# Projecting 32 sample tokens through four column groups of TensorE, beside the first prompt tile

## What is computed

```python
D_MODEL, SEQ, DEC_BATCH, DEC_SEQ = 1024, 1024, 8, 4
u = rmsnorm(h, attn_pre_g)
qa, kva, qi, ki, wi, qb, kb, vb, g_a, g_b = jnp.split(u @ w_in, cuts, axis=-1)
qa = rope(qa.reshape(B, T, H_A, DH_A), pos)          # rope: [x1*cos - x2*sin, x1*sin + x2*cos]
kv_a = jnp.stack([rope(kva[:, :, 0], pos), kva[:, :, 1]], axis=2)
qi = rope(qi.reshape(B, T, N_IDX, D_IDX), pos)
ki = rope(ki.reshape(B, T, 1, D_IDX), pos)[:, :, 0]
qb, kb = rope(qb, pos), rope(kb, pos)                # as heads of 64 columns
# samples: indexer scores over 8192 cached keys + 4 new ones, top 256 of them
score = einsum('bqh,bqhs->bqs', wi * N_IDX**-0.5, relu(einsum('bqhd,bsd->bqhs', qi, kidx) * D_IDX**-0.5))
_, sel = lax.top_k(score, 256)
```

## Time and profile before

| | |
|---|---|
| median of three runs | 3236.38 us |
| the profiled execution | 3238.8 us, its span 3237.3 us |
| PE busy | 2876.3 us (89% of the span) |
| VectorE busy | 1461.4 us (45%) |
| ScalarE busy | 588.2 us (18%) |
| GpSimd busy | 678.3 us (21%) |
| moved by DMA | 708.73 MB, mean 219 GB/s |

### The profile page before, as it was taken

One profiled execution on the slowest core, in us unless ns is written; L12 is line 12 of the kernel. 1 busy time (PEld: TensorE's weight loads), 2 busy tenths in 40 slices (PEclk: granted clock), 3 DMA queues, 4 the chain that ended last, 5 costly groups with the idle time before them and its releaser, 6 DMA issues. The chain is left out here.

```text
span 3237.3 us, 69341 instructions
## 1 busy us (share of the span) xinstructions
PE 2876.3 (89%) x26593; PEld 2020.4 (62%) x26593; DVE 1461.4 (45%) x3004; ACT 588.2 (18%) x1308; POOL 678.3 (21%) x1192
## 2 busy tenths in 40 slices
PE   8998979998789669999978889999798799998698
PEld 4764534665466446666755567766566576675698
DVE  2337858996788354333343443323433632002211
ACT  2431112001566110101011110010100201001101
POOL 0131003001100001133332433333333333430000
PEclk9999989999899889999998999999899899999799
DMA  7575239422500757789888988888888896662586
GB/s 226 148 226 181 79 117 305 128 79 87 164 8 18 223 182 245 241 299 315 297 303 271 310 297 276 308 305 302 300 282 276 268 300 235 223 204 91 174 266 197
DMA packets 419892, 708.73 MB, mean 219 GB/s; under 512 B 67985, under 2 KB 230193, under 8 KB 419442
## 3 DMA queue, kind: packets, MB, share of 16 engines
q1 hardware_dynamic: 330674, 470.65, 44.5%
q0 software_dynamic: 75456, 232.86, 21.7%
q10 hardware_dynamic: 13440, 0.85, 0.3%
HBM read 660.01 MB, written 92.13 MB: 232 GB/s over the span
## 5 line engine op out<-in xcount | busy, mean ns | idle before, releaser
L1458 PE MATMUL sa_t<-tw_z,tw_w 128*128 128x304 f32 x2496 | 679.8, 428 | 14.8 <-DVE tw_z L1535 10.7
L1458 PEld LDWEIGHTS sa_t<-tw_z,tw_w 128*128 128x128 f32 x2496 | 470.5, 192 | 195.3 <-issue 44.4
L1736 POOL DMA_DIRECT2D sa_ring_v<-cache_b_kv x512 | 275.2, 537 | 1211.5 <-PE sa_o L1865 850.4
L1458 PE MATMUL sa_t<-tw_x,tw_w 128*128 128x304 f32 x1440 | 406.0, 438 | 43.4 <-DMA tw_w<-packed 37.8
L1976 DVE STREAM_TRANSPOSE sa_key_b<-sa_ring_k 128x2048 f32<-128x2048 f32 x128 | 294.9, 2307 | 263.9 <-PE sa_s L1798 194.1
L1458 PEld LDWEIGHTS sa_t<-tw_x,tw_w 128*128 128x128 f32 x1440 | 277.5, 197 | 151.5 <-issue 64.6
L414 PE MATMUL pr_acc<-pr_w,pr_u_t 128*128 128x512 f32 (+1 forms) x720 | 288.1, 548 | 3.8 <-DVE pr_row L574 3.7
L1737 POOL DMA_DIRECT2D sa_ring_va<-cache_a_kv x512 | 274.2, 536 | 54.1 <-issue 27.0
L874 PE MATMUL sel_g<-sel_u,sel_gw 128*128 128x352 f32 x768 | 227.5, 459 | 0.0
L1798 PE MATMUL sa_s<-sa_key_b,sa_q_pad 32*32 32x256 f32 x8192 | 191.9, 416 | 26.1 <-DVE sa_key_b L1976 19.3
L874 PEld LDWEIGHTS sel_g<-sel_u,sel_gw 128*128 128x128 f32 x768 | 145.8, 190 | 81.9 <-issue 0.8
(11 more groups left out here) (336 smaller groups left out, 3499.7 us busy)
## 6 DMA issues: line engine op xcount, KB each, us to landing
sa_ring_k<-cache_b_kv SPq DMA_DIRECT2D x512, 256.0 KB, 4.0
sa_ring_v<-cache_b_kv POOLq DMA_DIRECT2D x512, 256.0 KB, 6.3
tw_w<-packed SPq DMA_DIRECT2D x228, 512.0 KB, 6.5
tp_w<-packed SPq DMA_DIRECT2D x76, 512.0 KB, 4.3
sa_ring_ka<-cache_a_kv SPq DMA_DIRECT2D x512, 64.0 KB
sa_ring_va<-cache_a_kv POOLq DMA_DIRECT2D x512, 64.0 KB, 6.2
packed<-w_gate_up POOLq DMA_DIRECT2D x44, 512.0 KB, 13.7
tw_w<-packed SPq DMA_DIRECT2D x48, 256.0 KB, 7.5
```

Source lines behind the costliest of these rows:

```text
L1458: ins = pe.matmul(bank[:, 0:self.width], self.w[:, at % self.SLOTS, k - lo, :], moving[:, k, :], start=(k == 0), stop=(k == depth - 1))
L1736: pool.dma_start(ring_v[:, n % RING, :], rows_of(cache_b, page, 1)).then_inc(v_in[n // 4 % 2], 16)
```

## The change

Tile 0 is no longer padded to 128 rows in the projection.

- **Four column groups.** Each chunk of 512 columns is cut into four of 128. For each of the eight slices of the contraction, four matmuls with a stationary operand of 128 x 32 (the 32 tokens) go to the array's column groups at 0, 32, 64 and 96, and stream 128 columns each. The result of one chunk is a block of 128 partitions (group, token) x 128 columns; the four large chunks fill one bank of 512 columns, borrowed from the selection's `dots[0]`. The chunk of 68 columns is written to a corner of the bank `once`.
- **One tile to rotate and turn.** VectorE rotates all four chunks at once with a cos/sin table repeated over the four groups (`trig_new`, four more small loads), and copies the unrotated values back over one block. PE turns four blocks and one of 64 columns instead of 16; ScalarE copies them out in five copies. The rows and heads of the 32 tokens leave in eight and four stores instead of four and one.
- **Tile 1 gets its own input buffer.** Its `x` and `ple` are loaded into the `rank` buffer (free until the ranking) right behind tile 0's, ahead of the weights. Its `square`, `mean`, `root` and `normalise` come right after tile 0 is turned. VectorE waits for all five table loads before them.
- **The order.** `first` now holds both tiles whole, chunk by chunk in turn; `units` begins with tile 2, so that `share` is smaller.

```diff
-    first = begin(0) + [u for c in range(4) for u in chunk(0, c)] + begin(1) + chunk(0, 4)
-    first += chunk(1, 0) + turn_heads(0) + chunk(1, 1)
-    units = chunk(1, 2) + chunk(1, 3) + begin(2) + chunk(1, 4)
+    first = begin(0) + chunk(0, 0) + begin(1) + chunk(1, 0) + chunk(0, 1) + chunk(1, 1) + chunk(0, 2) + chunk(0, 3)
+    first += chunk(1, 2) + chunk(0, 4) + chunk(1, 3) + turn_heads(0) + chunk(1, 4)
+    units = begin(2)
...
+        trig_new = ph.sb("trig_new", [P, 1, DH])
...
+        new_rows, new_ki = dots[0][:].rearrange("p s q -> p (s q)"), once[0:QS, 384:452]
+        def x_of(p):
+            return rank[:, 0:D] if p == 1 else x[:]
...
             load_x(0)
             sp.dma_start(gain[:], a["attn_pre_g"].partition_broadcast(P)).then_inc(gain_in, 16)
+            load_x(1)
             for c, (lo, hi) in enumerate(chunks):
                 sp.dma_start(w[:, :, lo:hi], ...).then_inc(w_in[c], 16)
                 if c == 0:
                     sp.dma_start(trig[:], ...).then_inc(trig_in, 16)
+                    for g in range(4):
+                        sp.dma_start(trig_new[g * QS:(g + 1) * QS, 0, :], a["trig"][SEQ:TOK, :]).then_inc(trig_in, 16)
...
             def project_chunk(slot):
+                if p == 0:
+                    if part == 0:
+                        pe.wait_ge(w_in[c], 16)
...
+                    for k in range(part * KC // PARTS, (part + 1) * KC // PARTS):
+                        if c == 2:
+                            ins = pe.matmul(new_ki, u_t[:, 0, k, 0:QS], w[:, k, lo:hi], start=(k == 0), stop=(k == KC - 1))
+                            continue
+                        for g in range(4):
+                            at = (c if c < 2 else c - 1) * P
+                            ins = pe.matmul(new_rows[g * QS:(g + 1) * QS, at:at + P], u_t[:, 0, k, 0:QS], w[:, k, lo + g * P:lo + (g + 1) * P],
+                                            start=(c == 0 and k == 0), stop=(k == KC - 1), tile_position=(0, g * QS), skip_group_check=True)
...
             def turn_head(slot):
+                if p == 0:
+                    if g == 0:
+                        pe.wait_ge(new_roped, 2)
...
+                    for j in range(4):
+                        ins = pe.transpose(turn[n % 2][:, j, :], row[:, 0, j * P:(j + 1) * P], ident[:])
...
+            def new_out(c):
+                if c == 2:
+                    dve.wait_ge(new_done, 1)
+                    nc.vector.tensor_copy(row[0:QS, 0, 576:580], new_ki[:, 64:68])
+                    rotate(new_ki[:, 0:64], row[0:QS, 0, 512:576], trig[0:QS, TILES:TILES + 1, :], slice(0, QS), 64).then_inc(new_roped, 1)
+                elif c == 4:
+                    dve.wait_ge(new_done, 2)
+                    rotate(new_rows, row[:, 0, 0:512], trig_new[:], slice(0, P), 512)
+                    dve.drain()
+                    nc.vector.tensor_copy(row[QS:2 * QS, 0, P:2 * P], new_rows[QS:2 * QS, P:2 * P]).then_inc(new_roped, 1)
...
-            dve.wait_ge(trig_in, 16)
+            dve.wait_ge(trig_in, 80)
...
+                elif slot == ("begin", 0, 4):
+                    mean(1)
+                    normalise(1)
```

More of the change, by code:

```diff
@@ L120, in turn_heads, with turned_heads @@
     def turn_heads(p):
-        return [[("heads", p, g) for g in range(4)]]
+        return [[("heads", p, g) for g in range(4 if p else 2)]]
+    def turned_heads(p):
+        return ("heads", p, 3 if p else 1)
     def cost_of(unit):
@@ L236, in project @@
         w_in = [ph.sem(f"w_in{c}") for c in range(5)]
-        x_in = ph.sem("x_in")
+        x_in = [ph.sem(f"x_in{c}") for c in range(2)]
         sumsq_ready, meansq_ready, std_ready = ph.sem("sumsq"), ph.sem("meansq"), ph.sem("std")
@@ L341, in _ @@
                     store_rows(slot[1])
-                elif slot[0] == "heads" and slot[2] == 3:
+                elif slot[0] == "heads" and slot == turned_heads(slot[1]):
                     store_heads(slot[1])
@@ L419, in turn_head @@
                 _, p, g = slot
+                if p == 0:
+                    n = turns[slot]
+                    if g == 0:
+                        pe.wait_ge(new_roped, 2)
+                    pe.wait_ge(turn_copied, n - 1)
+                    if g:
+                        pe.transpose(turn[n % 2][0:DH, 0, 0:QS], row[0:QS, 0, 512:576], ident[0:QS, 0:QS]).then_inc(turned, 1)
+                        return
+                    for j in range(4):
+                        ins = pe.transpose(turn[n % 2][:, j, :], row[:, 0, j * P:(j + 1) * P], ident[:])
+                    ins.then_inc(turned, 1)
+                    return
                 if g == 0:
-                    pe.wait_ge(roped, 5 * p + 5)
+                    pe.wait_ge(roped, 5 * p)
                 turn_group(slot, [row[:, p % 2, c:c + P] for c in pair_cols[4 * g:4 * g + 4]])
@@ L484, in begin_out @@
                     act.wait_ge(ut_stored, 16 * (p - 1))
[L485 removed]
+                    act.wait_ge(*((chunk_done, 5 * (p - 2)) if p > 2 else (new_done, 2)))
                 if g == 2 and p:
@@ L493, in heads_out @@
                 if g == 0 and p:
-                    act.wait_ge(heads_stored, 32 * p - 16)
-                if g == 1 and p:
+                    act.wait_ge(heads_stored, 32 * (p - 1) + 64)
+                if p == 0:
+                    bank = turn[turns[slot] % 2]
+                    act.wait_ge(turned, turns[slot] + 1)
+                    if g:
+                        nc.scalar.copy(heads[0:DH, 7, 0:QS], bank[0:DH, 0, 0:QS]).then_inc(turn_copied, 1)
+                        return
+                    nc.scalar.copy(heads[:, 4, 0:QS], bank[:, 1, 0:QS])
+                    nc.scalar.copy(heads[:, 5:7, 0:QS], bank[:, 1, 2 * QS:4 * QS].rearrange("p (j t) -> p j t", t=QS))
+                    nc.scalar.copy(heads[:, 0:4, 0:QS], bank[:, 0, :].rearrange("p (j t) -> p j t", t=QS))
+                    nc.scalar.copy(heads[:, 8:16, 0:QS], bank[:, 2:4, :].rearrange("p c (j t) -> p (c j) t", t=QS)).then_inc(turn_copied, 1)
+                    return
+                if g == 1:
                     cols = slice(tiles[p] * P, (tiles[p] + 1) * P)
@@ L524, in _ @@
                     begin_out(slot)
+                    if slot[1:] == (0, 4):
+                        square(1)
+                        root(1)
                 elif slot[0] == "heads":
                     heads_out(slot)
-                elif slot[0] == "chunk" and slot[1] + 1 < NTILE:
+                elif slot[0] == "chunk" and 0 < slot[1] < NTILE - 1:
                     if slot[2:] == (0, PARTS - 1):
@@ L682, in _ @@
                     _, p, c, part = slot
-                    if part == PARTS - 1:
+                    if part == PARTS - 1 and p:
                         chunk_out(p, c)
+                    elif part == PARTS - 1:
+                        new_out(c)
+                    if p == 0:
+                        continue
                     if p + 1 < NTILE and (c, part) == (0, PARTS - 1):
```

83 lines of the change are left out of this document (51 added, 32 removed).

## The result

The changed kernel takes 3276.8 us (median of 4 runs, 3269.3 to 3286.4) where the kernel before, run beside it, takes 3235.4 (4 runs). The ratio is 1.0128, with a 95% interval of 1.0101 to 1.0155: 41 us slower, where 12 us faster was forecast. The profiled execution took 3269.3 us with a span of 3267.7, against 3238.8 and 3237.3 before.

What follows compares the result with a forecast made beforehand. PE bounds the turned keys and dots and takes turns with VectorE in the count rounds. +0.8 - 3.4 + 0.8 - 8.5 - 1.7 = -12.0 us: 3226.8 us profiled, 3224 against the median; range 3215 to 3236 us.

Steps and rivals of the forecast that it cites:

- After it no phase depends on the absolute time, so that what the stage gains is what the kernel gains.: After the barrier ending the changed stage: the stage's gain, forecast at 12.0 us, passes whole to the kernel.
- The slow one: Rival, first 60 us: column groups' weight loads run one after another, 47 us more than forecast, 3271 us; chance 0.06.
- Up to the new dots: Kernel start to the first new dots: heads at 56.2 us, new dots at 67.2 us, 0.8 later than before.
- my lower bound of 63.6: Earliest forecast start of the new dots, in us: full clock and 1.8 us a samples' chunk.
- heads after 60 us: Sign of a wrong forecast, at the start: PE's heads later than 60 us, where 54 to 58 was expected.
- The clock at the start: Before the heads: PE's idling lowers the clock, costing 2.2 us (0 to 6.5), ending inside the first prompt chunk.
- the first rival: First 60 us: groups' weight loads in a row, 0.217 us a record, 13.9 us a chunk, 3271 us; chance 0.06.
- Turned keys and dots: From 66.4 to 229.8 us: four fewer 512-column matmuls, -3.4 us; a longer low clock, +0.8 us.
- The idle stretch: From 229.8 to 251.9 us: PE's work stays hidden behind the wait for the flat scores, no change.
- Count rounds: From 251.9 to 425.3 us: less PE work, limited by VectorE's chain, 8.5 us less (bounds 9.9 and 4).
- the rival of VectorE's bound: Count rounds: VectorE becomes the bound, rounds gain only 4 us, total gain 7.5 us, 3229 us; chance 0.17.
- The end: Behind the last count: PE has 8 matmuls of 512 columns for 10, 1.7 us less.

Runs made afterwards that it cites:

- 28 pads: 28 tiny unused 32x32 matmuls added on TensorE at the first stage's end: to the changed kernel, 3229.5 us; to that kernel with tile 1's turned x buffered separately, 3213.6 us.
- -53: Instruction-block borders 53 records ahead of the kernel before's in sample_attend: the changed kernel as it is, 3276.8 us; with a separate buffer for tile 1's turned x, 3264.4 us.
- +19: Block borders 19 records behind the kernel before's: the changed kernel with 28 tiny unused matmuls added at the first stage's end, 3229.5 us.
- tile 1's own buffer: Changed kernel with tile 1's turned x in eq instead of the shared xp_t: 3264.4 us, ratio 1.0087; with 28 tiny unused matmuls added, 3213.6 us, ratio 0.9944.
- the kernel before at +22: Kernel before with 53 tiny unused 32x32 matmuls added at the first stage's end, block borders 22 records behind: 3225.2 us, ratio 0.9986.

## Why the prediction was wrong

- **"After it no phase depends on the absolute time, so that what the stage gains is what the kernel gains."** This is the step that failed, and it carries all of the 30.5 us by which the profiled executions differ. The first half held: with 28 pads the part takes 1898.1 us when it starts at 1085.5 and 1898.5 when it starts at 1070.8. The second half did not follow. How long a later phase takes depends on how many instructions stand ahead of it: 1936.5 us with the borders at -53, 1898.1 with the same kernel's at +19. No rival of mine had this. The slow one (groups' weight loads in a row, 3271 us) came near the time by accident: its mechanism did not happen.
- **"Up to the new dots": +0.8 us, measured +13.7.** The terms were nearly right, and a wait was missing. The samples' chunk was priced at 2.1 us and takes 1.9 (the first 2.72, at a mean granted clock of 0.69); the weights at 16.8 were there at 15.6; tile 1's beginning started at 19.15, not 20.8. What I left out is queued behind the weights on SyncE: I priced tile 1's beginning from a row in which its buffer was long free, and named the landing of the "two stores of 1.2 MB" only for tile 2's input, not for ScalarE, which waits for the second of them. With that wait gone the dots came at 61.9 and 63.8, about my lower bound of 63.6. Of the signs of being wrong that I had named, heads after 60 us came true: 70.89, for a forecast of 56.2. From the heads to the dots it took 9.2 us (70.89 to 80.12), not 11.0.
- **The clock at the start:** 2.2 us, measured more. The granted clock was 0.50 from 18.30 to 22.90 us and, behind the missed wait, from 38.39 to 42.00. In all PE worked some 11 us at the lower level before the dots, which is an estimated 5.5 us. It is part of the 13.7 us, and most of it goes with the wait: with tile 1's own buffer the level was the lower one for none of the time before the dots, or for 3.4 us (with 28 pads).
- **The rule of the Trainium skill against the column groups** (TensorE: Matmul & The Clock Gate, "The mechanism") is what the first rival worked out at 0.217 us a record. The record takes 29.4 ns with neighbours in other column groups (1.88 us for 64), and 93 ns with neighbours in the same one. That all groups share their rows did not keep the loads from being hidden.
- **Turned keys and dots:** -3.4 + 0.8 = -2.6, measured -5.5. The 0.8 had the wrong sign. The clock fell behind the dots again, but came back by 88.3 us, after 6.8 us at the lower level, where before it had been 13.7 us (until 81.0). At half speed this is an estimated 3.4 us less.
- **The idle stretch:** 0, measured -3.1 (20.7 for 23.8).
- **Count rounds:** -8.5, measured -4.4, which is the size that the rival of VectorE's bound had (4 us). VectorE waits for PE in 16 rounds again, 21.9 us in all, where it was 20.5. In the waits view from 240 to 430 us of the changed kernel, PE waits for VectorE five times; the first, 7.8 us, is the one for the flat scores, and the other four, 4.2 us, are rounds that VectorE ends last. Before there were no such rounds (one wait, 10.6 us). That VectorE's bound is all of the missing 4 us is not shown:

```profile
PE pr_once L516 <- DVE pr_flipped L718: 12.0, 5, 7.8
```

```profile
PE pr_once L460 <- DVE pr_flipped L637: 10.6, 1, 10.6
```

- **The end:** -1.7, measured +0.2.

The sum for the stage was -12.0 and came out at +0.8 (470.73 for 469.88). With the missed wait gone the next stage starts at 456.89 us, 13.0 ahead of before, close to the sum, though its terms were not each right. With borders nearly alike the change is worth nothing measurable: 3229.5 us with 28 pads at +19, against 3225.2 for the kernel before at +22, ratios to before of 0.9998 (0.9974 to 1.0022) and 0.9986 (0.9963 to 1.0009). So the loss of 41 us is the position, and the expected gain went into the wait for `xp_t`: with its own buffer the same change at the same position has 0.9944 (0.9923 to 0.9966), 0.4% (some 13 us) below the kernel before at +22.

## What to carry to other kernels

When a change adds or drops instructions on TensorE, look first at idle time with no releaser in phases that it does not touch; if it stands at distances of some 127 records, compare versions only at the same position of the blocks, by adding free pads, before judging the change itself. When work is pulled to the start of a kernel, follow every buffer that it writes to the store that frees it, and the store to its place on the queue: here one store behind the weights cost 15.5 us. Matmuls in column groups should change the group at every step.

## What was not expected of the hardware

- TensorE's stream comes in packets of 16.4 KB, 256 instructions each (512 more instructions, two more packets). At some borders the packet starts late (at most 2.8 us before the engine runs dry), and the engine stops for up to 3.7 us. It goes on 1.15 to 1.62 us after the packet's end, at all 184 such cuts. Most of them (161) stand behind a block that was used up in 4.6 us or less, but some behind slower ones, of up to 14 us. By position this is 16 to 53 us of cuts in a kernel of 3.2 ms, and 1.5% of its time.
- The effect turns on 26 matmuls 600 us ahead of the place where it shows: ratio 1.0154 from 1.8 us of work, behind which the next stage starts only 1.1 us later (470.99 for 469.88).
- Four column groups of 32 columns on the same rows: 29.4 ns a record in turn, 93 ns one group at a time.
